# Queries and keys of two attention layers projected and rotated by features, placed by DMA, in groups of four heads

## The reference, cut to what matters

```python
def rope(x, pos):                       # per head of 64: x1, x2 are its halves of 32
    return concatenate([x1 * cos - x2 * sin, x2 * cos + x1 * sin])

# layer 1: 16 heads in each of 3 groups (window, dilation) = (128, 1), (512, 4), (2048, 16)
proj = h @ w_in                         # 1024 -> 3*3072 + 1024
q, k = rope(q, pos), rope(k, pos)
o_g, lse_g = windowed attention of group g over keys t, t-d, ..., t-window
o = sum_g softmax(lse)_g * o_g;  y = (o * silu(gate)) @ w_out

# layer 2: 8 heads, each with two maps of 64 and values of 128
q, k = rope(q, pos), rope(k, pos)
a = softmax(q1 k1') - lam * softmax(q2 k2');  o = rmsnorm(a @ v) ...
```

## Time and profile before

| | |
|---|---|
| median of 3 runs | 2835.04 us (2834.3 to 2835.27) |
| the profiled execution | 2832.68 us, its span 2831.4 us |
| TensorE busy | 2751.7 us, 97% of the span |
| VectorE, ScalarE, GpSimd busy | 42%, 39%, 39% |
| DMA | 268.90 MB, mean 95 GB/s |
| granted clock of TensorE | 0.994 over the run |
| layer 1 | 0 to about 703 us |
| layer 2 | about 703 to 989 us |

### The profile page before, as it was taken

One profiled execution on the slowest core, in us unless ns is written; L12 is line 12 of the kernel. 1 busy time (PEld: TensorE's weight loads), 2 busy tenths in 40 slices (PEclk: granted clock), 3 DMA queues, 4 the chain that ended last, 5 costly groups with the idle time before them and its releaser, 6 DMA issues.

```text
span 2831.4 us, 37369 instructions
## 1 busy us (share of the span) xinstructions
PE 2751.7 (97%) x14201; PEld 2220.0 (78%) x14201; DVE 1181.5 (42%) x2569; ACT 1095.8 (39%) x2037; POOL 1112.0 (39%) x894
## 2 busy tenths in 40 slices
PE   7999999999999999999999999999999999999998
PEld 6787878787878877776788888887777678888887
DVE  3343333344455355433335424265543333542425
ACT  3444434443455344352323424233435232342421
POOL 4323333334343443332355444444333235544443
PEclk9999999999999999999999999999999999999999
DMA  5332322223222232233243323223222324332321
GB/s 175 92 84 77 88 83 83 82 84 105 75 67 63 78 120 75 75 91 106 66 175 114 104 90 102 92 80 120 75 75 91 111 70 167 113 105 90 104 89 60
DMA packets 241397, 268.90 MB, mean 95 GB/s; under 512 B 16830, under 2 KB 191522, under 8 KB 240452
## 3 DMA queue, kind: packets, MB, share of 16 engines
q1 hardware_dynamic: 241220, 266.51, 30.7%
HBM read 247.52 MB, written 18.94 MB: 94 GB/s over the span
## 4 chain that ended last, share of the span: by engine, by line
PE 89%; DVE 5%; ACT 2%; issue 2%; POOL 1%; SPq 0%; DMA 0%; DVEq 0%; ACTq 0%
PE banks L1562 47%; PE banks L1559 27%; PE banks L1696 2%; DVE AR L2249 2%; PE banks L1645 1%; PE banks L1580 1%; PE banks L1803 1%; PE banks L1679 1%; PE banks L1595 1%; PE banks L1716 1%; PE banks L1851 1%; POOL WS L2820 1%; PE banks L1664 1%; PE banks L1767 1%; PE banks L1781 1%
## 5 line engine op out<-in xcount | busy, mean ns | idle before, releaser
L2820 POOL TENSOR_TENSOR WS<-WR,WS 128x512 fp32r<-128x512 f32 (+2 forms) x804 | 1010.2, 1291 | 1458.8 <-ACT WS L1907 1458.8
L1562 PE MATMUL banks<-WS,UT 128*128 128x512 f32 (+1 forms) x5424 | 1204.5, 370 | 10.3 <-DVE UT L2249 8.6
L1562 PEld LDWEIGHTS banks<-WS,UT 128*128 128x128 f32 x5424 | 894.8, 190 | 195.7 <-issue 43.5
L1559 PE MATMUL banks<-UT,WS 128*128 128x512 f32 (+1 forms) x2832 | 668.7, 395 | 0.7 <-ACT AR L2082 0.7
L1559 PEld LDWEIGHTS banks<-UT,WS 128*128 128x128 f32 (+1 forms) x2832 | 529.5, 189 | 125.6 <-issue 15.4
L1907 ACT ACTIVATE WS<-WR 128x1024 fp32r<-128x1024 f32 (+1 forms) x408 | 396.9, 1023 | 210.2 <-PE banks L1562 167.7
L1562 PE MATMUL banks<-WS,AT 128*128 128x512 f32 x1296 | 308.2, 396 | 0.0
L1562 PEld LDWEIGHTS banks<-WS,AT 128*128 128x128 f32 x1296 | 242.6, 188 | 58.4 <-ACT WS L1907 0.7
L2249 DVE TENSOR_TENSOR AR<-AR 128x256 f32<-128x256 f32 (+2 forms) x173 | 156.0, 920 | 12.0 <-ACT AR L2150 7.2
L2760 DVE SCALAR_TENSOR_TENSOR AR<-banks,AR 128x511 f32<-128x511 f32 x84 | 63.0, 750 | 218.8 <-ACT AR L2218 218.8
L2835 POOL TENSOR_TENSOR SM<-SM 128x1 f32<-128x1 f32 (+2 forms) x44 | 48.0, 1091 | 248.7 <-DVE SM L2736 105.9
(11 more groups left out here) (220 smaller groups left out, 2636.0 us busy)
## 6 DMA issues: line engine op xcount, KB each, us to landing
WR<-in_w_in SPq DMA_DIRECT2D x112, 512.0 KB, 3.6
WR<-in_w_up SPq DMA_DIRECT2D x88, 512.0 KB, 3.5
WR<-in_dil_w_in SPq DMA_DIRECT2D x256, 128.0 KB, 2.5
WR<-in_w_down SPq DMA_DIRECT2D x40, 512.0 KB, 3.7
WR<-in_dil_w_in SPq DMA_DIRECT2D x16, 512.0 KB, 4.0
WR<-in_diff_w_in SPq DMA_DIRECT2D x32, 256.0 KB, 3.1
WR<-in_diff_w_in SPq DMA_DIRECT2D x16, 512.0 KB, 3.7
spill<-AR SPq DMA_DIRECT2D x32, 256.0 KB, 2.1
```

What stands on the lines that cost most here:

```text
L1559: mm = pe.matmul(B[bank][0:c, :], w[part][:, kk, g * P:g * P + c], act[:, other, kk, :], start=start, stop=stop)
L1562: mm = pe.matmul(B[bank][:, off:off + n], act[:, other, before_k + kk, g * P:g * P + P], w[part][:, kk, :], start=start, stop=stop)
L2820: ge.tensor_tensor(slot(i, 1)[:, s], raw(i)[:, s], slot(i, 0)[:, s].bitcast(F32), ALU.subtract).then_inc(lo_p.sem, 1)
```

## The change: what it does

The tiles are cut anew. Layer 1 goes by groups p = 0 to 3 of four heads: one wide tile l1v (values of groups 1 and 2), and seven tiles of 256 columns: queries and keys of the three groups and l1w. Layer 2 has a wide l2v for p = 0 and 2, and for each p a tile of queries and one of keys. In a query or key tile the features are stationary and the 512 tokens move: two banks with 128 features by 512 tokens. The split gathers the weight columns (pieces of 32) so that both halves of a head's rotation stand on the same partition, one in each bank. `rope` is then for each bank two products of width 512 from PSUM with a table, and after the second bank two operations of width 512 in SBUF. A new step `spread` on SP sends the result with six DMAs to its places, on the partitions that the scores read. For queries and keys of these layers the transposes and ScalarE's copies are gone; the hybrid blocks keep theirs (and lines of `pairs` and `part` are simplified for them alone).

The units of layer 1 are ordered anew too: all near units (group 0) of four heads, then all their far ones. Projections of groups 1 and 2 stand beside the near units, those of the next four heads' values, group 0 and l1w beside the far ones. The first project is no longer run alone. Where attention of the earlier heads has to be finished first, the main generator yields without a projection. R_L1 and R_L2 change. The tables of cosine and sine are 128 x 512 each, one pair for layer 1, another for layer 2, loaded by two more DMAs of 512 KB; four buffers for `near` values and row maxima are doubled.

```diff
-R0, R1, R2, R3, R_L1, R_L2, R_G1, R_G2 = 0.994, 1.147, 1.512, 0.54, 0.92, 0.935, 1.38, 1.19
+R0, R1, R2, R3, R_L1, R_L2, R_G1, R_G2 = 0.994, 1.147, 1.512, 0.54, 0.76, 1.1, 1.38, 1.19
...
-    for p in range(8):
-        c = p * 128
-        wide(f"l1a{p}", w, c, 3072 + c, 1024 + c, 4096 + c)
-        if p % 2 == 0:
-            out.append((f"l1w{p}", KC, 256, [(0, cols(w, 6144 + c))]))
-        wide(f"l1b{p}", w, 2048 + c, 5120 + c, 7168 + c, 8192 + c)
+    for p in range(4):
+        c = 256 * p
+        wide(f"l1v{p}", w, 7168 + c, 8192 + c)
+        for name, o in (("q0", 0), ("k0", 3072), ("w", 6144), ("q1", 1024), ("k1", 4096), ("q2", 2048), ("k2", 5120)):
+            out.append((f"l1{name}{p}", KC, 256, [(0, cols(w, o + c))]))
...
-        wide(f"l2a{p}", w, 256 * p, 1024 + 256 * p)
-        out.append((f"l2v{p}", KC, 256, [(0, cols(w, 2048 + 256 * p))]))
+        if p % 2 == 0:
+            wide(f"l2v{p // 2}", w, 2048 + 256 * p)
+        for name, o in (("q", 0), ("k", 1024)):
+            out.append((f"l2{name}{p}", KC, 256, [(0, cols(w, o + 256 * p))]))
...
-    return [(p, far, i) for p in range(8) for far in range(2) for i in range(NB)]
+    return [(p, far, i) for pair in range(4) for far in range(2) for p in (2 * pair, 2 * pair + 1) for i in range(NB)]
...
-    def turned_heads(self, *where):
-        def deal(i, unit):
-            if where[0] == "1b":
-                self.step("copy", i, unit, "1v", where[1])
-            self.step("rope", i, unit, *where)
-            self.soon(4, lambda: self.step("pairs", i, unit, *where))
-        return deal
+    def rotated(self, name):
+
+
+        def deal(i, t):
+            self.step("rope", i, t)
+            if t:
+                self.soon(4, lambda: self.step("spread", i))
...
         def project(p):
-            yield from self.wide(f"l1a{p}", self.turned_heads("1a", p), fresh=(p == 0),
-                                 hold=lambda: p >= 2 and p - 2 not in attended)
-            if p % 2 == 0:
-                yield from self.token_major(f"l1w{p}", self.plain("copy", "1w", p))
-                self.soon(10, lambda: self.step("to_natural", p))
-            yield from self.wide(f"l1b{p}", self.turned_heads("1b", p), by=2)
-            self.soon(5, lambda: projected.add(p))
+            yield from self.wide(f"l1v{p}", self.plain("copy", "1v", p), fresh=(p == 0))
+            if p == 0:
+                self.step("lambda")
+                self.soon(8, lambda: self.step("rope_table"))
+            while p > 0 and (2 * p - 1, 0) not in attended:
+                yield 1
+            for name in ("q0", "k0"):
+                yield from self.rotated(f"l1{name}{p}")
+            yield from self.token_major(f"l1w{p}", self.plain("copy", "1w", p))
+            self.soon(3, lambda: self.step("to_natural", p))
+            self.soon(6, lambda: projected.add((p, 0)))
+            while p > 0 and (2 * p - 1, 1) not in attended:
+                yield 1
+            for name in ("q1", "k1", "q2", "k2"):
+                yield from self.rotated(f"l1{name}{p}")
+            self.soon(8, lambda: projected.add((p, 1)))
 
         def attention():
             units = l1_units()
...
-            for p in range(1, 8):
+            for p in range(4):
                 yield from project(p)
 
         late = []
-        self.drain(project(0))
-        self.step("lambda")
-        self.soon(8, lambda: self.step("rope_table"))
         att = attention()
...
         def project(p):
-            yield from self.wide(f"l2a{p}", self.turned_heads("2", p), fresh=(p == 0),
-                                 hold=lambda: p >= 2 and p - 2 not in attended)
-            yield from self.token_major(f"l2v{p}", self.plain("copy", "2v", p))
-            self.soon(2, lambda: projected.add(p))
+            if p % 2 == 0:
+                yield from self.wide(f"l2v{p // 2}", self.plain("copy", "2v", p), fresh=(p == 0))
+            while p >= 2 and p - 2 not in attended:
+                yield 1
+            for name in "qk":
+                yield from self.rotated(f"l2{name}{p}")
+            self.soon(8, lambda: projected.add(p))
 
         def attention():
...
+        def by_heads(i):
+            return tiles[i][0][:3] in ("l1q", "l1k", "l2q", "l2k")
+
+        def head_part(i, v, g):
+
+
+            f = raw(i)[:, 1024 * v:1024 * v + 1024].rearrange("p (a f c) -> p a f c", f=4, c=32)
+            o = 1024 * g + 512 * v
+            return f[:, :, 1:3, :] if g else f[:, :, ::3, :], slice(o, o + 512)
...
+                            if by_heads(i):
+                                c = 1024 * g + P * kk
+                                mm = pe.matmul(B[bank][:, :], slot(i, part)[:, c:c + P], act[:, other, kk, :],
+                                               start=start, stop=stop)
...
+                    i, t = a
+                    k = rotations.index(i)
+                    name = tiles[i][0]
+                    d = rotating(i)
+                    src, to_cos, to_sin = B[order.bank[i, t][0]], d[:, t, :], rope_part[:, 1 - t, :]
+                    cos_t, sin_t = rope_cos, rope_sin
+                    if name[:2] == "l1" and name[3] == "0":
+                        to_cos, to_sin = (v.rearrange("p (l r) -> p r l", r=4) for v in (to_cos, to_sin))
+                        src, cos_t, sin_t = (v.rearrange("p (r l) -> p r l", r=4) for v in (src, cos_t, sin_t))
+                    if t == 0:
+                        if name == "l1q00":
+                            ve.wait_ge(far_in, 16)
+                        if name == "l2q0":
+                            ve.wait_ge(nat_in, 16)
+                        if k > 0:
+                            ve.wait_ge(roped.sem, roped.at[rotations[k - 1]])
+                        if k > 1:
+                            ve.wait_ge(*there(rotations[k - 2]))
+                    ve.wait_ge(proj.sem, proj.at[i, t])
+                    tt(to_cos, src, cos_t, ALU.mult)
+                    tt(to_sin, src, sin_t, ALU.mult).then_inc(rope_read.sem, 1)
+                    if t:
+                        ve.wait_ge(rope_read.sem, rope_read.at[i, t])
+                        tt(d[:, 0, :], d[:, 0, :], rope_part[:, 0, :], ALU.add)
+                        tt(d[:, 1, :], d[:, 1, :], rope_part[:, 1, :], ALU.subtract).then_inc(roped.sem, 1)
...
+                elif kind == "spread":
+                    i, = a
+                    name, sent = tiles[i][0], there(i)[0]
+                    sy.wait_ge(roped.sem, roped.at[i])
+                    if name[:2] == "l1" and int(name[4]) > 0:
+                        sy.wait_ge(scored.sem, scored.at["1", l1_last(2 * int(name[4]) - 1, int(name[3] != "0"))])
+                    if name in ("l2q0", "l2q1"):
+                        sy.wait_ge(normed.sem, normed.at["u", NB - 1])
+                    if name[:2] == "l2" and int(name[3]) > 1:
+                        sy.wait_ge(scored.sem, scored.at["2", 8 * (int(name[3]) - 2) + 7])
+                    for e in range(2):
+                        d, s = rotated_to(i, e), rotating(i)
+                        sy.dma_start(d[0:32, :], s[64 * e:64 * e + 32, 0, :]).then_inc(sent, 16)
+                        sy.dma_start(d[32:96, :], s[64 * e:64 * e + 64, 1, :]).then_inc(sent, 16)
+                        sy.dma_start(d[96:128, :], s[64 * e + 32:64 * e + 64, 0, :]).then_inc(sent, 16)
+
...
-                    sy.wait_ge(w1_out, 32 * (p // 2 + 1))
-                    sy.dma_start(w1_of(p), w1_turn[p // 2].rearrange("(b p) c -> p b c", p=P)).then_inc(w1_in, 16)
+                    sy.wait_ge(w1_out, 32 * (p + 1))
+                    sy.dma_start(w1, w1_turn[p].rearrange("(b p) c -> p b c", p=P)).then_inc(w1_in, 16)
...
+                        if by_heads(i):
+                            for g in range(2):
+                                src, to = head_part(i, v, g)
+                                x = se.activation(slot(i, 0)[:, to].rearrange("p (a f c) -> p a f c", f=2, c=32), src,
+                                                  ACT.Copy)
+                            x.then_inc(hi.sem, 1)
...
+                    if by_heads(i):
+                        src, to = head_part(i, v // 2, v % 2)
+                        low, high = (slot(i, q)[:, to].rearrange("p (a f c) -> p a f c", f=2, c=32) for q in (1, 0))
+                        ge.tensor_tensor(low, src, high.bitcast(F32), ALU.subtract).then_inc(lo_p.sem, 1)
```

More of the change, by code:

```diff
@@ L355, in wide @@
                 self.open(name, early=not fresh)
-            self.bank[i + half, b] = ((4, 5, 0, 1)[b - first] if fresh and name != "l1a0" else (start + b) % 4, 0)
+            self.bank[i + half, b] = ((4, 5, 0, 1)[b - first] if fresh and name != "l1v0" else (start + b) % 4, 0)
             for k in (0, 2):
@@ L606, in main @@
         def main():
-            for p in range(1, 4):
+            for p in range(4):
                 yield from project(p)
         late = []
-        self.drain(project(0))
         att = attention()
@@ L944, in build @@
```

(11 more changed lines are left out.)

281 lines of the change are left out of this document (127 added, 154 removed).

## The result

| | before | changed |
|---|---|---|
| median of the runs | 2834.67 us (2834.06 to 2835.27, 4 runs) | 2856.23 us (2850.78 to 2858.15, 4 runs) |
| ratio | | 1.0073, 95% interval 1.0055 to 1.009 |
| the profiled execution, its span | 2832.68, 2831.4 | 2857.84, 2856.5 |
| granted clock of TensorE over the span | 0.994 | 0.985 |

The time lies above the forecast (2829) and above the end of its range (2850). The four runs of the changed kernel scatter over 7 us, at clocks of 0.985 to 0.987; those of the kernel before scatter over 1 here, but over 6 (2832.05 to 2837.76) in the 18 that the first experiments were compared with. Every median in this document leaves out runs in the chip's slow state, of which there were two: 3403.26 us (clock 0.749) for e3_scores_spaced and 3917.03 us (0.646) for the kernel before.

A forecast was written before the change was run, and what follows sets the result against it. The prediction took TensorE to bound both layers: 41.5 us saved less 34.9 us of new waits gives 6.6 us off the profiled 2832.7, 2826.1, or 2829 as a median after 2.4 and rounding; range 2807 to 2850.

The forecast's parts named there:

- What leaves TensorE: TensorE's savings from transposes, layer 2's values, fewer projection runs, rotation waits and layer 2's start: 41.5 us in sum.
- the removed waits: TensorE no longer waits for VectorE's rotation at transposes (3.6 us) or at the start of layer 2 (3.8 us).
- layer 2's values: In layer 2, 16 runs of 24 matmuls of width 256 become 12 of width 512, saving 1.8 us.
- the breaks: Projection runs in both layers fall from 319 to 223; 70 breaks of 0.12 us saved, less 0.07 each: 3.5 us.
- Every new wait of TensorE is paid in full: TensorE bounds both layers, so each new wait there lengthens the span by its idle time; 34.9 us added.
- item 6: Near scores wait for group 0's values through DRAM, 1.6 us at each of four p: 6.4 us.
- sign of failure: Forecast wrong if TensorE's idle time in the first 980 us grows by less than 15 or more than 45 us.
- Items 1 to 5: New TensorE waits: position table 3, layer 2's first scores 8, pair 1's end 4, gates 6, l1w tile ends 3 us.
- Item 7: Layer 2 ends later by an out product, squares and norm (1.5); maxima and copies behind rotations (3): 4.5 us.
- Costs that the trace did not show: Spreads landing in 3.0 us, 32-column gathers at plain cost, VectorE sums beside GpSimd; plain values kept, up to 8 us range.
- rival B: GpSimd's `lo` on pieces of 32 takes twice its 1.35 us, adding 18 us: 2847; chance 0.24.
- Rival A: New waits mostly covered, 12 us added instead of 34.9: 2806; chance 0.22.

The follow-up runs named there:

- the first experiments: The earliest follow-up runs, single edits of the changed kernel or of the kernel before, timed as medians against runs of the kernel before on the same chip.
- e3_scores_spaced: Changed kernel with extra yields after the first scores of layer 2, so 12 projections stand between each of the first three pairs: 2850.52 us, ratio 1.0058.
- v7: Changed kernel with l1w first, layer 2's first scores spaced, position table later, query and key tiles in steps of 6 matmuls, new ratios: 2802.81 us.
- v9: v7 with one number changed, R_G1 1.25 instead of 1.1: 2798.64 us, ratio 0.9873.

## Why the prediction was wrong, by its own steps

- **What leaves TensorE**: right in sum. 41.5 us had 34.1 of work, measured 32.6 (rest column), with the transposes confirmed by themselves at 27.1 against 25.7 without breaks; the removed waits went too. How the other 5.5 us divide between layer 2's values and the breaks isn't settled: v7 put breaks back and its rest did not grow.
- **"Every new wait of TensorE is paid in full"**: the step that failed. It took the idle time as the whole price of a wait. The waits of 2.7 us and more were in most cases paid once in full and then again by half speed behind them. 13 stretches of low clock cost 26.2 us where the kernel before had 3.2. The term of 23.0 us is more than three times what the sum needed to change sign (6.6), and it was in none of the rivals. It alone would have put the forecast at 2829 + 23 = 2852, out of its range; the rest of the miss is mostly item 6. Nor could the prediction's own sign of failure see it: idle time grew by 34.7 us, inside its 15 to 45. It could have been read from the kernel before: the clock behind its only such wait in these layers after the start.
- **Items 1 to 5** (table 3, first scores of layer 2 twice 4, end of pair 1 there 4, gates 6, out products 3): 3.5, 3.6 twice, 3.7, about 7.4, and about 0.7 three times. Places and sizes held.
- **Item 6**, near scores, 6.4 us: place right, size not; measured 13.8. For the first p the read back was issued 5.6 us after ScalarE's copy began, as reckoned, but took 6.1 to land and not 4.5, between weight loads (0.97 of the DMA engines busy at 94 to 96 us). For p = 1 it was issued 8.9 us after (225.34 to 234.23), since SP stood for two `lo` and not for one, and GpSimd began them only at 229.75, behind ScalarE's split.
- **Item 7**, 4.5 us: measured about 6.9, of which 4.5 are three waits of 1.51 at the first far transposes that I had not listed one by one.
- **Costs that the trace did not show.** `lo` on pieces of 32 columns: 1373 ns against 1353 for plain ones, so rival B's mechanism is excluded, and that its 2847 lay nearer to the result than my 2829 is chance. Products of the rotation 784 ns against 0.68 us, sums 897 on average against 0.69, with 3.39 for two in e3. Spreads land in 2.0 and 2.4 us.

```profile
L2296 DVE TENSOR_TENSOR AF<-banks,AF 128x512 f32<-128x512 f32 x128 | 93.8, 784 | 203.3 <-PE banks L1595 203.3
L2296 DVE TENSOR_TENSOR AF<-AF 128x512 f32<-128x512 f32 x64 | 54.8, 897 | 1.1
...
L2863 POOL TENSOR_TENSOR WS<-WR,WS 128x512 fp32r<-128x512 f32 x128 | 171.5, 1373 | 291.6 <-ACT WS L1952 291.6
L2865 POOL TENSOR_TENSOR WS<-WR,WS 128x512 fp32r<-128x512 f32 x124 | 163.6, 1353 | 242.5 <-ACT WS L1956 242.5
```

- **Rival A**, waits mostly covered, 2806: not so in the changed kernel; it is what v7 to v9 make of it by order alone.
- What stays open: why waits of the same length and place were followed by a fall in some kernels and not in others; and which places fell in the runs that weren't profiled.

## What to carry to other kernels

Price a wait of the matmul engine with the clock behind it: ask for the granted clock in the few microseconds after the longest waits that the old kernel already has, and add what it cost there to each new wait of such a length. Here that also held for the waits of 2.71 us, and for about half of those of 2.1 to 2.2. Where such a wait can't be avoided, matmuls whose result is thrown away are worth more than nothing: 15 of them at each of four places gave back about 10 us. And when a change coarsens the steps in which two streams are interleaved, look at who stands next to whom: here the change itself was worth 33 us of work, lost it to waits and clock, and gave it back (2834 to about 2799, 1.3%) when projections went in steps of 6 matmuls again, with values first and ratios to suit.

## What the runs showed of the hardware

Waits of TensorE of 2.7 us and more were in most cases followed by half clock that cost 1.3 to 3.3 us, most often 1.7 (ten of ten at 2.71 us, seven of ten at 3.19, eleven of eleven from 3.4 up for DMA or the table), waits of 2.1 to 2.2 in 7 cases of 15, and waits of 1.51 us ahead of far transposes in none of 18. Four 128x128 transposes between matmuls cost 0.42 us, while each lasted 0.27. A read back of 512 KB took 3.8 us to land when issued ahead of weight loads and up to 6.1 between them. Gathering pieces of 32 contiguous columns slowed GpSimd's subtraction by 1.5% only.
